# Two edits of a two-layer diffusion backbone: column-group sums of the modulation accumulators, and last down products with tokens on the partitions

## The chip, the cores and the metric

The kernel runs on one core of a Trainium2 chip. The metric is device time in microseconds (us) from launch to end. TensorE (PE) multiplies, VectorE (DVE) and ScalarE (ACT) work element by element, GpSimd (POOL) and SyncE (SP) mostly issue DMAs here. PE's weight loads have rows of their own (PEld). Every product of the bulk is done in three passes of a split float type, so that it has nearly float32 accuracy.

## The reference

Two layers over 256 latent tokens and 256 context tokens, 1024 channels each:

```python
# per layer; h = modulated RMSNorm; scale, shift and gate come from silu(c) @ w_mod + b_mod
x = x + 0.5 * gate1 * swiglu(h1, ffn1_w_gate, ffn1_w_up, ffn1_w_down)   # inner width 2816
x = x + gate_m * merge(token_mixers(h_m @ w_in), w_branch, w_out)
x = x + 0.5 * gate2 * swiglu(h2, ffn2_w_gate, ffn2_w_up, ffn2_w_down)
# after layer 1:
out = x * rsqrt(mean(x * x, axis=-1) + 1e-6) * final_norm               # latent tokens only
```

Context tokens go the same way with modulation vectors made from `c_ctx`. Behind the mixers of the last layer only latent tokens are left, so the last feed-forward block (ffn2 of layer 1) has 256 tokens.

## The kernel before

Activations lie with channels on partitions: `X` is 128 x 8 chunks x 512 tokens. Weights are handled in **units** of 128 x 1024 elements (512 KB). SP loads a unit into one of four `raw` slots. ACT copies it to `w_hi`, rounded to the split type (`split_hi`, L656), and DVE makes the rest `w_lo = raw - w_hi` (`split_lo`, L669). PE (`product`, L699) then does for each of its 8 rows of 128 channels two matmuls with `w_hi` as weights (L711 with the high part of the activations, L712 with their low part), and 8 more with `w_lo` (L717). `w_hi` and `w_lo` have two slots each: the unit after next can only be split when this one's matmuls have read them.

A feed-forward block has three **parts** of 8, 6 and 8 inner chunks (`PARTS`). A part is 16, 12 or 16 "up" units (gate and up products in turn, of h, with silu and product behind each pair) and then a "down" sweep of 8 units, one for each output chunk of 128 channels, with the part's inner chunks as rows. DVE adds each result times its gate to `X` (L1660). `inner_hi` comes from ACT (L1223) and `inner_lo` from DVE (L1622) behind each pair of up units. In the last sweep ACT also squares the new `X` chunk (L1173), POOL adds the squares up (L2112), and PE sums them over the partitions with a matrix of ones (L804, L806). Then follow the final norm (root, reciprocal, and the multiplication L1969), 16 transposes (L1161) that bring tokens to the partitions, four copies by ACT (L1545), and two DMAs out.

**Modulation.** silu(c) @ w_mod doesn't go over PE but for the first 16 chunks (`modulation`, L820, 32-column tiles on the four column groups of PE). The other 128 chunks, in 32 groups of 4, are loaded by POOL in the feed-forward blocks before they are needed. DVE multiplies and adds 8 rows of a group into `mac_acc` (`gstage` or `spread_odd`, L1645), for the context stream ACT scales (L1247) and POOL adds (L2019). What is left is to sum 128 partitions. `sum_macs` (L831) does it on PE behind fixed units (`sum_after`): for each chunk and stream one float32 matmul with 128 x 128 of the accumulator as weights and one column of ones as moving data (L847), which gives the 128 sums as a column of `bank[7]`. 24 groups have both streams (8 matmuls), 8 have one (4 matmuls). A float32 matmul is two records in the trace, one for each pass.

## Time and profile before

| | us |
|---|---|
| median of 3 runs (lowest to highest) | 2291.53 (2289.37 to 2294.31) |
| profiled execution, its own time | 2293.94 |
| its span in the trace | 2292.2 |
| PE busy, of the span | 2197.9 (96%) |
| DVE, ACT, POOL busy | 1473.0, 1006.3, 556.5 |
| DMA | 339.62 MB, mean 148 GB/s |

PE is busy nearly all the time, and its clock was granted at 0.986 of full speed on the mean. DVE is at 64% over the span. A row names the line of the kernel; for a matmul it reads out<-moving,weights. Start-to-start times of matmuls are the pace; a single matmul's own duration also has its latency and is longer than the pace.

### The profile page before, as it was taken

The numbers are of one execution on the slowest core, as the hardware profiler recorded it, in microseconds if no ns is written. First come the engines' busy times: TensorE is split into PE (matmuls) and PEld (weight loads), VectorE is DVE, ScalarE is ACT, GpSimd is POOL, SyncE is SP. The second block draws the span as 40 slices with busy tenths as digits, with TensorE's granted clock in tenths as the row PEclk, the third lists the DMA queues.
The fourth block names the chain that finished last, engine by engine and source line by source line (L and its number), as shares of the span: only waits on it lengthen the run. The fifth ranks groups of instructions, "written<-read, shape, count | busy, mean of one in ns | idle before, by whom it ended". The sixth has DMA issues, their size and how long they took to land. (4 is left out here: it accounts for less than half of the span.)

```text
span 2292.2 us, 32512 instructions
## 1 busy us (share of the span) xinstructions
PE 2197.9 (96%) x12273; PEld 1846.9 (81%) x12273; DVE 1473.0 (64%) x2102; ACT 1006.3 (44%) x1575; POOL 556.5 (24%) x566
## 2 busy tenths in 40 slices
PE   6999999999999988999999999999998999988998
PEld 3888888977666766988888898887888777888997
DVE  3877786783576457776666674445459558675554
ACT  3544444543455432553343453222245356634444
POOL 0556566420010011334443320000015001110000
PEclk8999999999999999999999999999999999999999
DMA  8566675633333335555445455545444445465663
GB/s 272 156 206 183 168 207 154 173 92 86 97 107 92 97 117 155 173 150 156 147 141 172 128 163 161 147 133 157 144 129 127 120 120 155 143 182 147 177 182 113
DMA packets 488576, 339.62 MB, mean 148 GB/s; under 512 B 13194, under 2 KB 460150, under 8 KB 488294
## 3 DMA queue, kind: packets, MB, share of 16 engines
q1 hardware_dynamic: 458240, 238.06, 36.3%
q0 software_dynamic: 28736, 95.30, 14.2%
q10 hardware_dynamic: 1446, 4.19, 0.5%
q8 instruction: 98, 1.61, 0.3%
q14 instruction: 56, 0.46, 0.1%
HBM read 325.92 MB, written 12.35 MB: 148 GB/s over the span
## 5 line engine op out<-in xcount | busy, mean ns | idle before, releaser
L677 DVE TENSOR_TENSOR w_lo<-raw,w_hi 128x1024 fp32r<-128x1024 f32 (+1 forms) x444 | 582.2, 1312 | 554.1 <-PE bank L717 363.1
L667 ACT ACTIVATE w_hi<-raw 128x1024 fp32r<-128x1024 f32 (+1 forms) x444 | 462.0, 1041 | 708.3 <-PE bank L712 372.3
L711 PE MATMUL bank<-h_hi,w_hi 128*128 128x512 f32 (+1 forms) x1856 | 647.3, 361 | 10.7 <-DVE h_lo L1559 10.6
L712 PE MATMUL bank<-h_lo,w_hi 128*128 128x512 f32 (+1 forms) x1856 | 639.0, 356 | 0.0
L711 PEld LDWEIGHTS bank<-h_hi,w_hi 128*128 128x128 f32 x1856 | 353.3, 190 | 63.4 <-issue 12.5
L717 PE MATMUL bank<-h_hi,w_lo 128*128 128x512 f32 (+1 forms) x1856 | 395.1, 355 | 3.7 <-DVE w_lo L677 3.7
L712 PEld LDWEIGHTS bank<-h_lo,w_hi 128*128 128x128 f32 x1856 | 353.7, 191 | 48.9 <-issue 0.5
L717 PEld LDWEIGHTS bank<-h_hi,w_lo 128*128 128x128 f32 x1856 | 313.8, 190 | 53.1 <-DVE w_lo L677 4.5
L711 PE MATMUL bank<-inner_hi,w_hi 128*128 128x256 f32 (+1 forms) x896 | 273.4, 327 | 11.9 <-DVE inner_lo L1622 11.6
L712 PE MATMUL bank<-inner_lo,w_hi 128*128 128x256 f32 (+1 forms) x896 | 270.4, 325 | 0.0
L711 PEld LDWEIGHTS bank<-inner_hi,w_hi 128*128 128x128 f32 x896 | 168.7, 188 | 31.1 <-DVE inner_lo L1622 15.8
L2000 POOL DMA_DIRECT2D wm<-in_w_mod_dram x128 | 92.8, 725 | 372.3 <-DVE gstage L1645 165.0
L726 PE MATMUL bank<-h_hi,w_hi 128*128 128x512 f32 (+1 forms) x512 | 169.7, 350 | 12.8 <-ACT wa L1418 7.7
L712 PEld LDWEIGHTS bank<-inner_lo,w_hi 128*128 128x128 f32 x896 | 168.4, 188 | 14.9
L727 PE MATMUL bank<-h_lo,w_hi 128*128 128x512 f32 (+1 forms) x512 | 165.1, 341 | 0.0
L717 PE MATMUL bank<-inner_hi,w_lo 128*128 128x256 f32 (+1 forms) x896 | 165.0, 324 | 0.0
L717 PEld LDWEIGHTS bank<-inner_hi,w_lo 128*128 128x128 f32 x896 | 135.2, 188 | 15.3
L1223 ACT ACTIVATE inner_hi<-wb 128x512 fp32r<-128x512 f32 (+1 forms) x88 | 50.9, 579 | 217.2 <-DVE wb L1618 217.2
L726 PEld LDWEIGHTS bank<-h_hi,w_hi 128*128 128x128 f32 x512 | 98.5, 192 | 47.2 <-ACT gstage L1418 19.1
L1645 DVE SCALAR_TENSOR_TENSOR gstage<-wm,cact,gstage 128x512 f32<-128x512 f32 x112 | 126.2, 1126 | 2.3
L1645 DVE SCALAR_TENSOR_TENSOR spread_odd<-wm,cact,spread_odd 128x512 f32<-128x512 f32 x112 | 123.3, 1101 | 2.3
L1660 DVE SCALAR_TENSOR_TENSOR X<-bank,gatev,X 128x256 f32<-128x256 f32 x192 | 87.9, 478 | 54.9 <-PE bank L717 54.9
(241 smaller groups left out, 2918.3 us busy)
## 6 DMA issues: line engine op xcount, KB each, us to landing
wm<-in_w_mod_dram POOLq DMA_DIRECT2D x128, 512.0 KB, 4.1
raw<-in_w_in_dram SPq DMA_DIRECT2D x108, 512.0 KB, 3.8
raw<-in_ffn_w_gate_dram SPq DMA_DIRECT2D x88, 512.0 KB, 4.3
raw<-in_ffn_w_up_dram SPq DMA_DIRECT2D x88, 512.0 KB, 3.9
raw<-in_ffn_w_down_dram SPq DMA_DIRECT2D x88, 512.0 KB, 4.0
raw<-in_ffn_w_down_dram SPq DMA_DIRECT2D x32, 384.0 KB, 3.4
raw<-in_w_out_dram SPq DMA_DIRECT2D x24, 512.0 KB, 4.0
raw<-in_w_mod_dram SPq DMA_DIRECT2D x16, 512.0 KB, 5.9
```

The lines of the kernel that those rows point to most:

```text
L667: act.activation(w_hi[n % 2][:, 0:unit.rows, :], raw[unit.slot][:, 0:unit.rows, :], ACT.Copy).then_inc(hi_made, 1)
L677: dve.tensor_tensor(w_lo[n % 2][:, 0:unit.rows, :], raw[unit.slot][:, 0:unit.rows, :], w_hi[n % 2][:, 0:unit.rows, :].bitcast(F32), ALU.su ...
L711: pe.matmul(psum, w_hi[s][:, row0 + k, :], hi, start=(k == 0), stop=False)
L712: mm = pe.matmul(psum, w_hi[s][:, row0 + k, :], lo, start=False, stop=False)
L717: mm = pe.matmul(psum, w_lo[s][:, row0 + k, :], rhs(k)[0], start=False, stop=(k == rows - 1))
L726: pe.matmul(psum, w_hi[s][:, k, :], h_hi[:, k, 0:n], start=(k == 0), stop=False)
L727: mm = pe.matmul(psum, w_hi[s][:, k, :], h_lo[:, k, 0:n], start=False, stop=False)
L1223: act.activation(inner_hi[:, bass.ds(i * 2 + j // 2, 1), 0:n], wb[:, (j // 2) % 2:(j // 2) % 2 + 1, 0:n], ACT.Copy).then_inc(inner_hi_made, 1)
L1645: ins = dve.scalar_tensor_tensor(out=acc, in0=row, scalar=cact[:, k, 0:1], in1=acc, op0=ALU.mult, op1=ALU.add)
L1660: ins = dve.scalar_tensor_tensor(out=X[:, d % DC, stream_cols(st)], in0=bank[4 + d % 2][:, stream_cols(st)], scalar=gatev[:, gate_i, d % D ...
L2000: wm_loaded[i % 3].done(pool.dma_start(wm[i % 3][:, :, :], w_mod[layer].rearrange("(k p) n -> p k n", p=P)[:, 2 * h:2 * h + 2, chunk * P:( ...
```

## The change

Two edits at once. **Sums.** `sum_macs` now issues four float32 matmuls per group, with 32 columns of ones as weights on the four column groups of PE and 256 columns (128 where there is one stream) of the accumulator as moving data; they fill `bank[6]` with rows of sums. One unit later ACT copies `bank[6]` to `mac_rows` (`copy_rows`), and one more unit later PE turns the rows to columns of `bank[7]` with two matmuls (one for one stream) of 128 x 128 as weights and 4 (8) columns of `pick8` (`turn_macs`).

**Last down products.** In ffn2 of layer 1 the down products have tokens on the partitions of the result. The activations (`inner_hi`, `inner_lo`, 128 tokens of one inner chunk) are the weights and 512 output channels of `w_hi` or `w_lo` the moving data. A unit is 2 inner chunks x 512 channels (half of the 1024), 8 + 6 + 8 = 22 units in place of 24. Four banks (two token halves by two channel halves) collect over all three parts, so that nothing is added to `X`. `X` itself is turned to tokens by 16 transposes before the block (`turn_residual`) and copied to `res` by ACT. At the end DVE multiplies by the gate row, adds `res` and multiplies by the final norm's row, ACT squares with a sum along the free axis, and both scale by the inverse root. The gate row and norm row are spread over the partitions by POOL's DMAs (`last_rows`), one through DRAM.

```diff
...
+def by_tokens(l, name):
+    return l == LAYERS - 1 and name in [(2, part) for part in range(len(PARTS))]
 def sweep_steps(l, name):
-    return DC * sweep_halves(l, name)
+    return PARTS[name[1]][1] if by_tokens(l, name) else DC * sweep_halves(l, name)
...
+            res = sb("res", [P, 2, D], F32, region)
+            gate_all = sb("gate_all", [P, D], F32, region)
+            fin_all = sb("fin_all", [P, D], F32, region)
...
+        RES_BANKS = [(1, 1, 3), (0, 0, 4), (0, 1, 5), (1, 0, 7)]
+        def token_units(l, part):
+            rows = PARTS[part][1]
+            return [(first["down", l, 2, part] + j, j // (rows // 2), j % (rows // 2)) for j in range(rows)]
+        scaled = (gstage, spread_odd)
...
+        mac_rows = (probs[:, 2, :], probs[:, 3, :])
-                sum_after.setdefault(u0 + int(pace * (i + 1)) + 2, []).append(g)
+                at_unit = u0 + int(pace * (i + 1)) + 2
+                sum_after.setdefault(at_unit, []).append(g)
+                copy_after.setdefault(at_unit + 1, []).append(g)
+                turn_after.setdefault(at_unit + 2, []).append(g)
...
+                        if by_tokens(l, (ffn, part)):
+                            for u, half, a in token_units(l, part):
+                                unit = units[u]
+                                sp.wait_ge(lo_made, units[u - SLOTS].product + 1)
+                                sp.dma_start(raw[unit.slot][:, :, :].rearrange("p r c -> p (r c)").rearrange("p (k n) -> p k n", k=2),
+                                             wd[l].rearrange("(c p) n -> p c n", p=P)[:, c0 + 2 * a:c0 + 2 * a + 2, half_cols(half)]
+                                             ).then_inc(loaded[unit.slot], 16)
+                            continue
...
             def sum_macs(u):
                 for g in sum_after.get(u, ()):
+                    n = GROUP * P // 2 if 1 in group_streams(g) else P
+                    mac_dve.wait(pe, (g, DC - 1))
+                    if 1 in group_streams(g):
+                        mac_pool.wait(pe, (g, DC - 1))
+                    if g > 0:
+                        pe.wait_ge(mac_rows_copied, g)
+                    for j in range(4):
+                        if 1 in group_streams(g):
+                            acc = mac_acc[g % 2][:, j % 2, :].rearrange("p (b h c) -> p b h c", b=2, h=2)[:, :, j // 2, :]
+                        else:
+                            acc = mac_acc[g % 2][:, 0, j * P:(j + 1) * P]
+                        mm = pe.matmul(bank[6][32 * j:32 * j + 32, 0:n], const("ones")[:, 0:32], acc, start=True, stop=True)
+                    mac_summed.done(mm, g)
+            def turn_macs(u):
+                for g in turn_after.get(u, ()):
                     l, chunk0 = MAC_GROUPS[g]
                     if g == 0:
                         vectors.wait(pe, (0, "in"))
...
                         vectors.wait(pe, (0, "gate"))
                     elif (l, chunk0) == (1, 5 * DC):
                         vectors.wait(pe, (1, "in"))
-                    mac_dve.wait(pe, (g, DC - 1))
+                    pe.wait_ge(mac_rows_copied, g + 1)
+                    c = mod_col(chunk0, 0)
                     if 1 in group_streams(g):
-                        mac_pool.wait(pe, (g, DC - 1))
-                    for s in group_streams(g):
-                        for q in range(GROUP):
-                            col = mod_col(chunk0 + q, s)
-                            mm = pe.matmul(bank[7][:, col:col + 1], mac_acc[g % 2][:, s, q * P:(q + 1) * P], const("ones")[:, 0:1],
+                        for b in range(2):
+                            mm = pe.matmul(bank[7][:, c + 4 * b:c + 4 * b + 4], mac_rows[g % 2][:, b * P:(b + 1) * P], const("pick8")[:, 0:8:2],
                                            start=True, stop=True)
-                    mac_summed.done(mm, g)
+                    else:
+                        mm = pe.matmul(bank[7][:, c:c + 8], mac_rows[g % 2][:, 0:P], const("pick8"), start=True, stop=True)
+                    mac_turned.done(mm, g)
...
+            def turn_residual(l):
+                pe.wait_ge(added, add_first[l, "out"] + sweep_steps(l, "out"))
+                vectors.wait(pe, (l, "rest"))
+                for t, half, b in RES_BANKS:
+                    for k in range(4):
+                        mm = pe.transpose(bank[b][:, k * P:(k + 1) * P], X[:, 4 * half + k, t * P:(t + 1) * P], const("ident"))
+                    res_turned.done(mm, b)
+            def down_by_tokens(l, part):
+                rows = PARTS[part][1]
+                last_part = part == len(PARTS) - 1
+                before = inner_first[l, 2, part]
+                if part == 0:
+                    pe.wait_ge(res_copied, len(RES_BANKS))
+                for u, half, a in token_units(l, part):
+                    s = units[u].product % 2
+                    wide_hi, wide_lo = (w[s][:, :, :].rearrange("p r c -> p (r c)").rearrange("p (k n) -> p k n", k=2) for w in (w_hi, w_lo))
+                    pe.wait_ge(hi_made, units[u].product + 1)
+                    last = last_part and a == rows // 2 - 1
+                    def hi_terms(t):
+                        for k in range(2):
+                            c = 2 * a + k
+                            if half == 0 and t == 0:
+                                pe.wait_ge(inner_lo_made, before + c + 1)
+                            begin = part == 0 and c == 0
+                            pe.matmul(bank[4 + 2 * t + half][:, :], inner_hi[:, c, t * P:(t + 1) * P], wide_hi[:, k, :], start=begin, stop=False)
+                            mm = pe.matmul(bank[4 + 2 * t + half][:, :], inner_lo[:, c, t * P:(t + 1) * P], wide_hi[:, k, :], start=False, stop=False)
+                        return mm
+                    def lo_terms(t):
+                        for k in range(2):
+                            c = 2 * a + k
+                            mm = pe.matmul(bank[4 + 2 * t + half][:, :], inner_hi[:, c, t * P:(t + 1) * P], wide_lo[:, k, :], start=False,
+                                           stop=last and k == 1)
+                        return mm
+                    if last:
+                        pe.wait_ge(lo_made, units[u].product + 1)
+                        hi_terms(0)
+                        tokens_done.done(lo_terms(0), (0, half))
+                        hi_terms(1).then_inc(hi_used, 1)
+                        mm = lo_terms(1)
+                    else:
+                        hi_terms(0)
+                        hi_terms(1).then_inc(hi_used, 1)
+                        pe.wait_ge(lo_made, units[u].product + 1)
+                        lo_terms(0)
+                        mm = lo_terms(1)
+                    mm.then_inc(unit_done, 1)
...
-            for t in range(2):
-                for half in range(2):
-                    for k in range(4 * half, 4 * half + 4):
-                        if t == 0:
-                            normed.wait(pe, ("final", k))
-                        mm = pe.transpose(bank[2 * t + half][:, (k % 4) * P:(k % 4 + 1) * P], X[:, k, t * P:(t + 1) * P], const("ident"))
-                    pe_start.done(mm, ("out", t, half))
...
+            def copy_rows(u):
+                for g in copy_after.get(u, ()):
+                    n = GROUP * P // 2 if 1 in group_streams(g) else P
+                    mac_summed.wait(act, g)
+                    if g >= 2:
+                        mac_turned.wait(act, g - 2)
+                    act.activation(mac_rows[g % 2][:, 0:n], bank[6][:, 0:n], ACT.Copy).then_inc(mac_rows_copied, 1)
+            def copy_residual(at_bank):
+                t, half, b = RES_BANKS[at_bank]
+                res_turned.wait(act, b)
+                act.activation(res[:, t, half_cols(half)], bank[b][:, :], ACT.Copy).then_inc(res_copied, 1)
+            def square_tokens(t, half):
+                res_added.wait(act, (t, half))
+                res_squared.done(act.activation(wa[:, t, :], res[:, t, half_cols(half)], ACT.Square, accum_out=ssq[:, t, half:half + 1]), (t, half))
+            def token_splits(l, part):
+                last_part = part == len(PARTS) - 1
+                for j, (u, half, a) in enumerate(token_units(l, part)):
+                    if last_part and j == 0:
+                        act.activation(early_root[:, 7:8], eps_col[:, 0:1], ACT.Sqrt)
+                    split_hi(act, units[u].product + 2)
+                    if last_part and j in (4, 5):
+                        square_tokens(j - 4, 0)
+                if last_part:
+                    for t in range(2):
+                        square_tokens(t, 1)
+                        res_summed.wait(act, t)
+                        res_root.done(act.activation(ssq[:, t, 2:3], ssq[:, t, 2:3], ACT.Sqrt, bias=eps_col[:, 0:1], scale=1.0 / D), t)
+                        res_inverse.wait(act, t)
+                        res_scaled.wait(act, (t, 0))
+                        act.activation(res[:, t, half_cols(0)], scaled[0][:, t, :], ACT.Identity, scale=ssq[:, t, 3:4]).then_inc(acts_finished, 1)
...
                 for i in range(PARTS[part][1] // 2):
+                    body(i)
                     if (l, ffn, part, i) == (0, 1, 0, 3):
                         modulation_vectors(0, "gate")
...
+            def add_tokens(t, half):
+                if (t, half) == (0, 0):
+                    row_loads.wait(dve, "all")
+                    dve.wait_ge(res_copied, len(RES_BANKS))
+                if t == 0:
+                    tokens_done.wait(dve, (t, half))
+                else:
+                    dve.wait_ge(unit_done, token_units(LAYERS - 1, 2)[4 * half + 3][0] + 1)
+                part = res[:, t, half_cols(half)]
+                gated.done(dve.tensor_tensor(wb[:, t, :], bank[4 + 2 * t + half][:, :], gate_all[:, half_cols(half)], ALU.mult), (t, half))
+                gated.wait(dve, (t, half))
+                res_added.done(dve.tensor_tensor(part, part, wb[:, t, :], ALU.add), (t, half))
+                res_added.wait(dve, (t, half))
+                res_scaled.done(dve.tensor_tensor(scaled[half][:, t, :], part, fin_all[:, half_cols(half)], ALU.mult), (t, half))
+            def finish_tokens(t):
+                res_squared.wait(dve, (t, 1))
+                res_summed.done(dve.tensor_tensor(ssq[:, t, 2:3], ssq[:, t, 0:1], ssq[:, t, 1:2], ALU.add), t)
+                res_root.wait(dve, t)
+                res_inverse.done(dve.reciprocal(ssq[:, t, 3:4], ssq[:, t, 2:3]), t)
+                res_inverse.wait(dve, t)
+                res_scaled.wait(dve, (t, 1))
+                dve.tensor_scalar(res[:, t, half_cols(1)], scaled[1][:, t, :], ssq[:, t, 3:4], None, ALU.mult).then_inc(dves_finished, 1)
+            def token_block(l, part):
+                last_part = part == len(PARTS) - 1
+                for j, (u, half, a) in enumerate(token_units(l, part)):
+                    if last_part and j in (4, 5):
+                        add_tokens(j - 4, 0)
+                    split_lo(dve, units[u].product + 2)
+                if last_part:
+                    for t in range(2):
+                        add_tokens(t, 1)
+                        if t == 1:
+                            finish_tokens(0)
+                    finish_tokens(1)
...
-            norm_invert(("final", 0), 0)
-            for k in range(DC):
-                normed.done(dve.scalar_tensor_tensor(out=X[:, k, 0:LAT], in0=X[:, k, 0:LAT], scalar=vec2[:, 0, V_FIN + k:V_FIN + k + 1],
-                                                     in1=rstd[:, 0:LAT], op0=ALU.mult, op1=ALU.mult), ("final", k))
...
+            def last_rows():
+                gate_row_stored.done(pool.dma_start(last_gates.rearrange("(c p) -> p c", p=P), gatev[:, 2, :, 0], allow_slow_non_contiguous=True), 0)
+                row_loads.done(pool.dma_start(fin_all[:, :], final_norm.rearrange("(a d) -> a d", a=1).to_broadcast([P, D])), 0)
+                gate_row_stored.wait(pool, 0)
+                row_loads.done(pool.dma_start(gate_all[:, :], last_gates.rearrange("(a d) -> a d", a=1).to_broadcast([P, D])), "all")
```

Below, what stands on PE and DVE at the places that matter. PE behind up unit 6 of the first part of ffn1, layer 0, before:

```order
L712 MATMUL bank<-h_lo,w_hi 128x512
L717 MATMUL bank<-h_hi,w_lo 128x512 x8
L847 MATMUL bank<-cst,gstage 128x1 x8
L711 MATMUL bank<-h_hi,w_hi 128x512
L712 MATMUL bank<-h_lo,w_hi 128x512
```

and in the change (line numbers are the new ones; `cst` holds the ones and `pick8`, `probs` holds `mac_rows`), first behind the same unit, then two units later:

```order
L766 MATMUL bank<-h_lo,w_hi 128x512
L771 MATMUL bank<-h_hi,w_lo 128x512 x8
L899 MATMUL bank<-gstage,cst 32x256 x4
L765 MATMUL bank<-h_hi,w_hi 128x512
L766 MATMUL bank<-h_lo,w_hi 128x512
```

```order
L766 MATMUL bank<-h_lo,w_hi 128x512
L771 MATMUL bank<-h_hi,w_lo 128x512 x8
L916 MATMUL bank<-cst,probs 128x4 x2
L765 MATMUL bank<-h_hi,w_hi 128x512
L766 MATMUL bank<-h_lo,w_hi 128x512
```

Eight matmuls of one moving column have become four of 256 columns on 32-column tiles, and two of four columns two units later.

The end of DVE's program, before (the last down sweep's end, then the final norm):

```order
L677 TENSOR_TENSOR w_lo<-raw,w_hi 128x1024
L1660 SCALAR_TENSOR_TENSOR X<-bank,gatev,X 128x256
L677 TENSOR_TENSOR w_lo<-raw,w_hi 128x1024
L1660 SCALAR_TENSOR_TENSOR X<-bank,gatev,X 128x256 x3
L1573 RECIPROCAL rstd<-rstd 128x256
L1969 SCALAR_TENSOR_TENSOR X<-X,vec,rstd 128x256 x8
```

and in the change, from the split of unit 6 of the last sweep's units 0 to 7:

```order
L731 TENSOR_TENSOR w_lo<-raw,w_hi 128x1024
L1845 TENSOR_TENSOR wb<-bank,gate_all 128x512
L1847 TENSOR_TENSOR res<-res,wb 128x512
L1849 TENSOR_TENSOR gstage<-res,fin_all 128x512
L731 TENSOR_TENSOR w_lo<-raw,w_hi 128x1024
L1845 TENSOR_TENSOR wb<-bank,gate_all 128x512
L1847 TENSOR_TENSOR res<-res,wb 128x512
L1849 TENSOR_TENSOR spread_odd<-res,fin_all 128x512
L1845 TENSOR_TENSOR wb<-bank,gate_all 128x512
L1847 TENSOR_TENSOR res<-res,wb 128x512
```

The additions of three whole 128 x 512 operations each now stand between the last splits and behind the last products; a reciprocal of 128 x 256 and eight multiplications are gone from the end.

## Rows read from the trace of the kernel before

**Rows 1.** The page: busy time and share of PE, and its granted clock in tenths.
```profile
PE 2197.9 (96%) x12273; PEld 1846.9 (81%) x12273; DVE 1473.0 (64%) x2102; ACT 1006.3 (44%) x1575; POOL 556.5 (24%) x566
...
PEclk8999999999999999999999999999999999999999
```
**Rows 2.** Stretch of ffn1, layer 0: busy PE, PEld, DVE, ACT, POOL, clock, DMA share, GB/s.
```profile
60.00:130.00 70.00, 69.98 (x347) 59.17 (x346) 60.63 (x57) 37.81 (x55) 40.24 (x32) 1.00 0.59 173
```
**Rows 3.** Timeline of PE at a group with two streams: start, us, engine, line, what.
```profile
93.46 1.84 PE L847 MATMUL bank<-cst,gstage 128*128 128x1 f32 x16
95.16 0.49 PE L711 MATMUL bank<-h_hi,w_hi 128*128 128x512 f32 x1
95.48 0.40 PE L712 MATMUL bank<-h_lo,w_hi 128*128 128x512 f32 x1
```
**Rows 4.** Timeline of PE, L717 of two units in turn, then a one-stream group.
```profile
1651.38 1.98 PE L717 MATMUL bank<-h_hi,w_lo 128*128 128x512 f32 x8
...
1656.82 1.98 PE L717 MATMUL bank<-h_hi,w_lo 128*128 128x512 f32 x8
1658.64 0.95 PE L847 MATMUL bank<-cst,gstage 128*128 128x1 f32 x8
```
**Rows 5.** Timeline of PE at the start: float32 passes, then four tiled matmuls.
```profile
40.97 0.38 PE L804 MATMUL bank<-wb,cst 128*128 128x256 f32 x1
41.19 0.59 PE L806 MATMUL bank<-wa,cst 128*128 128x256 f32 x2
41.71 1.07 PE L820 MATMUL bank<-raw,cact 128*32 128x512 f32 x8
```
**Rows 6.** Timeline of PE into and out of 64-column tiles; out of 64-row tiles.
```profile
680.52 0.39 PE L727 MATMUL bank<-h_lo,w_hi 128*128 128x512 f32 x1
680.83 0.64 PE L1088 MATMUL bank<-mod_row,x_tok 128*64 128x512 f32 x1
...
681.84 2.12 PE L736 MATMUL bank<-h_hi,w_lo 128*128 128x512 f32 x8
...
623.90 0.50 PE L726 MATMUL bank<-h_hi,w_hi 128*128 128x512 f32 x1
624.24 0.39 PE L727 MATMUL bank<-h_lo,w_hi 128*128 128x512 f32 x1
```
**Rows 7.** Timeline of PE in ffn2, layer 1: last L717 before each down sweep and in it.
```profile
2128.97 1.12 PE L717 MATMUL bank<-h_hi,w_lo 128*128 128x256 f32 x8
...
2153.33 1.12 PE L717 MATMUL bank<-inner_hi,w_lo 128*128 128x256 f32 x8
...
2187.88 1.12 PE L717 MATMUL bank<-h_hi,w_lo 128*128 128x256 f32 x8
...
2206.83 0.88 PE L717 MATMUL bank<-inner_hi,w_lo 128*128 128x256 f32 x6
...
2252.66 1.12 PE L717 MATMUL bank<-h_hi,w_lo 128*128 128x256 f32 x8
2256.80 0.39 PE L711 MATMUL bank<-inner_hi,w_hi 128*128 128x256 f32 x1 [1.35 <-DVE inner_lo L1622]
...
2277.75 1.12 PE L717 MATMUL bank<-inner_hi,w_lo 128*128 128x256 f32 x8
```
**Rows 8.** Groups by form on DVE and ACT: busy us, mean ns, idle before.
```profile
L1618 DVE TENSOR_TENSOR wb<-bank,wa 128x512 f32<-128x512 f32 x66 | 45.1, 683 | 0.0
...
L1852 DVE RECIPROCAL smax<-smax 128x1 f32<-128x1 f32 x72 | 11.7, 162 | 3.9 <-ACT probs L1444 1.3
...
L1446 ACT ACTIVATE smax<-sink,smax 128x1 f32<-128x1 f32 x24 | 6.8, 283 | 0.0
```
**Rows 9.** Timeline of DVE at the start of the last down sweep.
```profile
2254.28 1.23 DVE L677 TENSOR_TENSOR w_lo<-raw,w_hi 128x1024 fp32r<-128x1024 f32 x1 [1.82 <-ACT w_hi L667]
```
**Rows 10.** Chain of waits, its last piece: start, us, what.
```profile
2288.46 0.60 ACT out_rows L1545
```
**Rows 11.** Timeline of PE behind the output projection of layer 1.
```profile
2081.17 0.55 PE L784 MATMUL bank<-h_hi,w_hi 128*128 128x256 f32 x1 [4.15 <-DVE h_lo L1588]
```

73 lines of the change are left out of this document (54 added, 19 removed).

## The prediction

> **What bounds the kernel now.** I read the page first: PE is busy 96% of the span at a clock granted near full speed all along [rows 1]. So whatever shortens PE's own program is worth nearly all of itself, and an edit on another engine is worth nothing unless PE waits for it. Next the stretches: in ffn1 of layer 0, where the modulation groups lie thickest, PE is busy 69.98 of 70.00 us, DVE 60.63 (87%), ACT 37.81 (54%), the DMA engines 0.59 [rows 2]. PE sets the time there, but DVE isn't far. Then PE's timeline at the sums, at other changes of tile shape, and in ffn2 of layer 1, and last the end of the program, where PE has stopped and a chain of DVE, ACT and DMA is left.
>
> **Sums, removed.** At a two-stream group PE starts the first L847 at 93.46 and the next product at 95.16: 1.70 us for 16 records. The product's second matmul then comes 0.32 later [rows 3], where the pace is 5.44 / 24 = 0.227 (two L717 rows one unit apart, 1651.38 and 1656.82) [rows 4]: 0.10 more. That is 1.80 for a group. The busy time of those 16 records, 1.84, is 0.14 longer than the 1.70. At a one-stream group 8 records have 0.95 [rows 4], less 0.14 that is 0.81, with the 0.10 it is 0.91. All: 24 x 1.80 + 8 x 0.91 = 50.5 us. A record more costs (1.70 - 0.81) / 8 = 0.111.
>
> **Sums, added.** Do float32 matmuls on four column groups run beside each other? L820 does just this at the start: four matmuls of 512 columns with 32 columns of weights, 8 records, in 1.07 us, the last one's latency included [rows 5]. A pass of 256 columns on the whole array takes 41.19 - 40.97 = 0.22, so one of 512 takes 0.43, and 8 in turn would be 3.4 us. So they do. The price of the change of shape comes from the 64-column products: the last 128-column matmul starts at 680.52 and the first tiled one at 680.83, 0.31 and not 0.227, so 0.08 for going in; two passes of 512 columns then take 681.84 - 680.83 = 1.01 [rows 6], of which 0.15 is more than 2 x 0.43 and goes to the turnovers, the way out among them. After a way out, the next matmul but one is late as well, 624.24 - 623.90 = 0.34 for 0.227, 0.11 more [rows 6]. A group with two streams thus costs 0.08 + (2 x 0.22 + 0.15) + 0.11 = 0.78, and I add 0.02 for four tiles that can't start in the same instant: 0.80. The turn two units later is 4 records of the old kind: 1.70 - 12 x 0.111 = 0.37, and 0.10 behind it, 0.47. Sum 1.27 for 1.80, a gain of 0.53. With one stream: 0.08 + (2 x 0.11 + 0.15) + 0.11 + 0.02 = 0.58, and a turn of 2 records, 0.14 + 0.10: 0.82 for 0.91, a gain of 0.09. Together 24 x 0.53 + 8 x 0.09 = **13.4 us**. The bounds: if ways in and out cost nothing, a group is 0.34 cheaper still (11 us in all); if the four tiles run one after the other, the first rival below.
>
> The Trainium skill has a rule against this edit (TensorEngine Tiling (Array Packing), Tiling Modes): changing the tiling mode drains the engine. It gives no time for it. The trace agrees that there is a price, 0.08 in and some 0.2 out [rows 6], which the sum holds already. The same page's table (Overview) promises up to 4x for a dimension of 32 or less, and rows 5 show it.
>
> What else the edit adds: ACT copies 128 x 256 or x 128 per group, at most the 0.60 of a whole 512 [rows 10], 32 times in stretches where ACT is 46% idle [rows 2]; PE asks for the copy two units, 10.9 us, after the sums, so I cost it at nothing. If ACT were a unit late, each group would lose what it is late, which is the price if that cover is gone. DVE waits for the turn, not the sum, before it makes the vectors, but does so four units after the last turn it needs. The "gate" vectors move behind an up pair on DVE; the same work, before the sweep that uses them. Behind them DVE still has a whole unit (5.44) before the split is due. Queues of SP and POOL aren't moved past anything here.
>
> **Last down products, sweeps.** Three sweeps [rows 7]. Part 0: L717 of the last up unit starts at 2128.97, that of the last down unit at 2153.33, 24.36. Part 1: (2206.83 + 6 x 0.12) - (2187.88 + 8 x 0.12) = 18.71. In the change a unit is 12 matmuls of 512 columns, 12 x 0.227 = 2.72 us: 8 units 21.8, 6 units 16.3. Gain 2.6 + 2.4. It has two sources. 512 columns take 0.227, twice 256 take 0.24. And the old sweep's first unit needs all inner chunks at once, so it waits for the last `inner_lo`: 1.35 us of it in the last part [rows 7], somewhat over 1 in the others. The new first units need chunks 0 and 1 only; the last pair is asked for at the fourth (third) unit, 5 us or more later. Nothing takes that place. Of a unit's 2.72 DVE needs 1.23 for its split [rows 9], and it no longer adds to `X`.
>
> **The last sweep and the end.** Now from the end of up, 2252.66 + 8 x 0.12 = 2253.62, to 2292.2: 38.6 us. In the change, from that zero: unit 7 could start at 7 x 2.72 = 19.0. But unit 7 waits for its whole split before it starts, and DVE now has two additions of three operations of 0.68 [rows 8] between its last splits: it splits for unit 5 once unit 3 (done at 10.9) has gone and ACT has made the high part (11.8 to 13.0, by [rows 9]), adds to 15.1, splits for unit 6 to 16.3, adds to 18.3, splits for unit 7 to 19.5. So unit 7 starts at **19.5**, half a us late. Its first token half is done at 19.5 + 6 x 0.227 + 0.2 = 21.1, and DVE's three operations for it end at 23.2; the second half waits for them, to 25.2. Then the sum of squares (0.16), ACT's root (0.28), the inverse (0.16) [rows 8] with four handovers, 25.9; ACT scales in 0.60 [rows 10], 26.5. ACT's order puts the last square behind that: 27.1, sum, root and inverse again 27.8, scaled 28.4. From the last ACT operation to the span's end it was 2292.2 - (2288.46 + 0.60) = 3.1 [rows 10], with the same size of DMA: 31.5. Gain 38.6 - 31.5 = **7.1**. DVE's and ACT's tail is what is late next.
>
> **The turn of the residual.** 16 transposes are put where PE waits 4.15 us for the first `h_lo` (until 2081.17) [rows 11]. At the higher clock 128 float32 columns take 0.11 (half of 256 in [rows 5]), at the lower one 0.22, so they need 1.8 to 3.5 us. They fit. If they don't, it costs up to 1 us; if they keep the clock up, it gives a few tenths back. ACT copies them beside the first up units, 4 x 0.60 in 11 us. POOL's three DMAs have 170 us until they are needed.
>
> **Sum.** 13.4 + 2.6 + 2.4 + 7.1 = 25.5. From the profiled execution, 2293.94 - 25.5 = 2268.4. That execution was 2.4 above the median of the runs, so the median to expect is 2291.53 - 25.5 = **2266.0**.
>
> **Rivals.**
> - *The column groups don't overlap in this form.* Then a two-stream group has 8 passes of 0.22 in turn, 1.76 + 0.34 for the shapes + 0.47 = 2.57, and loses 0.77; a one-stream group has 0.88 + 0.34 + 0.24 = 1.46 and loses 0.55. 24 x 0.77 + 8 x 0.55 = 22.9 lost, 12.1 gained elsewhere: 2291.5 + 10.8 = 2302, slower. It decides once the four tiled matmuls of a two-stream group take over some 1.8 us and not 0.8. Rows 5 speak against it: same type, same weights' width, one bank. Chance 0.04.
> - *The sums' gain is hidden*, since DVE's multiply-and-adds set the pace once PE is quicker. For it: 87% in rows 2. Against: PE waited 0.02 of 70 us there, and DVE's share only rises to 89%. Then only 12.1 is left: 2279. Chance 0.07.
> - *The token sweeps don't gain*: splits come late, or the end's chain is as long as the old one. Then 13.4 and some: 2277. Chance 0.07. Against it: DVE is at less than half a unit in the sweeps.
> - *Neither does what it says* and the time stays within 0.2% (about what a measurement of this kernel can tell from no change): 0.02.
> - My forecast, both terms within a third of their size: 0.80.
>
> Faster by over 0.2% holds all but the first rival and the fourth, 0.94; slower 0.04. The range: 2260, where ways in and out cost half of what I take and the end is 1 us shorter, to 2276, where one of the two middle rivals is half true.
>
> **What would show it.** In the profile after: four tiled matmuls (8 records) in about 0.6 us and no L847; no wait of PE for `mac_rows` copies; down units of layer 1's ffn2 2.72 apart, with no gap at the first; PE idle under 1 us before the last unit; the last PE matmul of the last product some 9 us before the end, where it was 13.3. Wrong would be: tiled records one behind another, waits <-ACT `probs` on PE, or a clock below full in the last sweep.

## The result, and the profile after

| | before | after |
|---|---|---|
| median (lowest to highest), us | 2291.36 (2289.37 to 2294.31) | 2270.66 (2267.81 to 2273.47) |
| profiled execution, span | 2292.2 | 2266.0 |
| PE busy | 2197.9 | 2174.7 |

The ratio is 0.9909, with an interval of 0.9896 to 0.9922: 20.7 us faster, where I forecast 25.5. The spans differ by 26.2, but 5.1 of that lie before the first product (it starts at 48.69 before and 43.57 after), where the first loads come in; in the eleven kernels of the experiments it starts at 42.84 to 45.69. So I compare stretches from the first product on. Their bounds are the starts of the first matmuls of `first_pair` and `score`. So the first two columns hold the input products of a layer's mixers too, and "mixers" is what lies from a layer's first scores to its next feed-forward block. There neither edit touches anything but for the 16 transposes, which fill a wait. One execution each, us (differences in the text are of unrounded times):

| kernel | ffn1, layer 0 | ffn2 L0 and ffn1 L1 | mixers | last block to the end | sum |
|---|---|---|---|---|---|
| before | 546.7 | 898.2 | 587.6 | 211.0 | 2243.5 |
| after | 540.3 | 891.4 | 586.4 | 204.3 | 2222.4 |
| e1, sums alone | 541.0 | 890.9 | 584.8 | 210.6 | 2227.3 |
| e2, tokens alone | 545.8 | 898.3 | 585.4 | 204.2 | 2233.7 |
| e3, three more | 556.3 | 908.8 | 585.4 | 204.2 | 2254.7 |
| e4, banks | 540.3 | 889.7 | 585.8 | 204.2 | 2219.9 |
| e5, residual early | 540.5 | 891.4 | 586.1 | 200.7 | 2218.6 |
| e6, copy and vectors early | 537.4 | 891.3 | 585.3 | 203.1 | 2217.1 |
| e7, end order | 542.0 | 889.7 | 586.5 | 203.4 | 2221.6 |
| e8, 128 bytes on | 541.3 | 887.2 | 586.1 | 203.1 | 2217.6 |
| e9, all together | 536.4 | 888.6 | 584.4 | 199.0 | 2208.3 |
| e10, 256 bytes on | 540.3 | 891.4 | 586.0 | 203.0 | 2220.7 |
| e11, 64 bytes on | 540.9 | 888.1 | 585.4 | 203.5 | 2217.9 |

The 21.0 us between the first two rows are 6.4 + 6.8 in the stretches with the sums, 6.6 in the last block, and 1.2 that belongs to neither edit. The first two sections of the page after, beside [rows 1]:

```profile
PE 2174.7 (96%) x11925; PEld 1796.8 (79%) x11925; DVE 1474.5 (65%) x2085; ACT 1015.7 (45%) x1608; POOL 553.7 (24%) x563
...
PEclk9999999999999999999999999999999999999999
```

PE, at 96%, still bounds the kernel. Next the timeline of PE at the sums of one group and at the turn of another, which answers to [rows 3], and at the sums of a one-stream group:

```profile
88.40 0.64 PE L899 MATMUL bank<-gstage,cst 128*32 128x256 f32 x8
88.97 0.50 PE L765 MATMUL bank<-h_hi,w_hi 128*128 128x512 f32 x1
89.31 0.39 PE L766 MATMUL bank<-h_lo,w_hi 128*128 128x512 f32 x1
...
124.80 0.51 PE L916 MATMUL bank<-cst,probs 128*128 128x4 f32 x4
125.16 0.48 PE L765 MATMUL bank<-h_hi,w_hi 128*128 128x512 f32 x1
...
1638.80 0.42 PE L899 MATMUL bank<-gstage,cst 128*32 128x128 f32 x8
1639.16 0.50 PE L765 MATMUL bank<-h_hi,w_hi 128*128 128x512 f32 x1
```

Eight records of 256 columns are over in 0.57 us and the next matmul but one is 0.11 late (89.31 - 88.97 = 0.34). The turn has 0.36. That is the mechanism that I forecast, to 0.04 us. But at two groups of the first block PE waits for something. These are rows of DVE, ACT and PE around the first of them, and PE's row at the second:

```profile
98.67 0.68 DVE L1775 TENSOR_TENSOR wb<-bank,wa 128x512 f32<-128x512 f32 x1
...
99.38 0.63 ACT L1344 ACTIVATE inner_hi<-wb 128x512 fp32r<-128x512 f32 x1 [5.33 <-DVE wb L1775]
99.92 1.32 ACT L1409 ACTIVATE probs<-wm,cact 128x512 f32<-128x512 f32 x2
...
101.14 0.36 ACT L1360 ACTIVATE probs<-bank 128x256 f32<-128x256 f32 x1
...
101.65 0.58 PE L916 MATMUL bank<-cst,probs 128*128 128x4 f32 x4 [1.50 <-ACT probs L1360]
...
149.45 0.61 PE L916 MATMUL bank<-cst,probs 128*128 128x4 f32 x4 [0.94 <-DVE gatev L1895]
```

Read it from the bottom up. PE waits for ACT's copy L1360. ACT had been idle for 5.33 us, but the copy stands in its order behind `inner_hi`, which needs DVE's `wb`, and behind two scalings. This is one of the signs that the prediction had named for being wrong ("waits <-ACT `probs` on PE"), at one of 32 turns. The second wait, at 149.45, is for the "gate" vectors, which the change moved behind DVE's last multiply-and-adds of the part. In the last block the timeline of PE shows the largest wait:

```profile
2057.30 3.01 PE L958 MATMUL bank<-cst,X 128*128 128x128 f32 x16
2061.66 0.36 PE L838 MATMUL bank<-h_hi,w_hi 128*128 128x256 f32 x1 [1.35 <-DVE h_lo L1745]
...
2072.10 1.12 PE L771 MATMUL bank<-h_hi,w_lo 128*128 128x256 f32 x8
2075.25 0.38 PE L765 MATMUL bank<-h_hi,w_hi 128*128 128x256 f32 x1 [2.03 <-ACT res L1366]
...
2077.78 1.91 PE L771 MATMUL bank<-h_hi,w_lo 128*128 128x256 f32 x8
```

The 16 transposes fit in the gap, as forecast. But the fourth up unit needs bank 3, out of which ACT has not yet copied the residual. ACT's timeline shows what stands ahead of that copy (L1366):

```profile
2070.05 1.28 ACT L1341 ACT_TABLE_LOAD   x1
...
2074.30 0.42 ACT L1344 ACTIVATE inner_hi<-wb 128x256 fp32r<-128x256 f32 x1 [1.63 <-DVE wb L1775]
2074.62 0.58 ACT L1366 ACTIVATE res<-bank 128x512 f32<-128x512 f32 x1
```

It stands behind `inner_hi`, which waits for DVE's `wb`, and ahead of both ACT loads a table for silu. And behind the wait the same eight matmuls take 1.91 us and not 1.12. The windows of that stretch (columns as in [rows 2]) show why: behind the wait the clock was granted at 0.50, which is 1.2 GHz.

```profile
2073.40:2075.20 1.80, 0.00 (x0) 0.00 (x0) 1.29 (x3) 0.90 (x3) 0.00 (x0) 1.00 0.66 197
2076.70:2079.90 3.20, 3.20 (x17) 3.20 (x16) 0.81 (x2) 1.26 (x2) 0.00 (x0) 0.50 0.42 116
```

Now two token units in turn on PE, beside the sweeps in [rows 7]:

```profile
2118.92 1.08 PE L986 MATMUL bank<-w_lo,inner_hi 128*128 128x512 f32 x4
...
2121.70 1.10 PE L986 MATMUL bank<-w_lo,inner_hi 128*128 128x512 f32 x4
```

A unit takes 2.79 us on the mean, not 2.72. Last the chain of waits at the end, which answers to [rows 10]:

```profile
2258.86 0.69 DVE spread_odd L1849
...
2259.65 0.30 ACT ssq L1386
...
2260.18 0.72 ACT res L1389
2260.90 0.62 ACT wa L1371 x2
...
2262.26 0.72 ACT res L1389
```

ACT's second square (L1371) stands behind its first scaling (L1389), as forecast, but has an instruction more behind it that reads the sum out (x2), and a scaling takes 0.72, not 0.60.

### The profile page after: what moved, and what is told of

Same layout as the page of the kernel before. It is cut to its first block and busy times, and to the rows that moved or that the text cites. A ratio compares the mean times of both kernels' runs of the same rounds, so it can differ in the third digit from the quotient of the medians.

```text
span 2266.0 us, 31839 instructions
## 1 busy us (share of the span) xinstructions
PE 2174.7 (96%) x11925; PEld 1796.8 (79%) x11925; DVE 1474.5 (65%) x2085; ACT 1015.7 (45%) x1608; POOL 553.7 (24%) x563
## 3 DMA queue, kind: packets, MB, share of 16 engines
q0 software_dynamic: 29056, 96.35, 14.5%
## 5 line engine op out<-in xcount | busy, mean ns | idle before, releaser
L765 PE MATMUL bank<-h_hi,w_hi 128*128 128x512 f32 (+1 forms) x1856 | 650.5, 362 | 13.1 <-DVE h_lo L1716 11.0
L765 PE MATMUL bank<-inner_hi,w_hi 128*128 128x512 f32 (+1 forms) x720 | 229.9, 340 | 7.7 <-DVE inner_lo L1779 7.4
L766 PE MATMUL bank<-inner_lo,w_hi 128*128 128x512 f32 (+1 forms) x720 | 225.7, 334 | 0.0
L765 PEld LDWEIGHTS bank<-inner_hi,w_hi 128*128 128x128 f32 x720 | 135.5, 188 | 28.8 <-DVE inner_lo L1779 11.0
L766 PEld LDWEIGHTS bank<-inner_lo,w_hi 128*128 128x128 f32 x720 | 135.6, 188 | 13.8
L771 PE MATMUL bank<-inner_hi,w_lo 128*128 128x512 f32 (+1 forms) x720 | 139.3, 334 | 0.0
L771 PEld LDWEIGHTS bank<-inner_hi,w_lo 128*128 128x128 f32 x720 | 112.1, 188 | 14.9
L1817 DVE SCALAR_TENSOR_TENSOR X<-bank,gatev,X 128x256 f32<-128x256 f32 x168 | 76.2, 477 | 49.5 <-PE bank L771 49.5
```

Source lines behind the costliest of these rows:

```text
L765: pe.matmul(psum, w_hi[s][:, row0 + k, :], hi, start=(k == 0), stop=False)
L766: mm = pe.matmul(psum, w_hi[s][:, row0 + k, :], lo, start=False, stop=False)
L771: mm = pe.matmul(psum, w_lo[s][:, row0 + k, :], rhs(k)[0], start=False, stop=(k == rows - 1))
L1817: ins = dve.scalar_tensor_tensor(out=X[:, d % DC, stream_cols(st)], in0=bank[4 + d % 2][:, stream_cols(st)], scalar=gatev[:, gate_i, d % D ...
```

## The experiments

**Each edit alone (e1, e2).** e1 is the kernel before with the diff's `sum_macs`, `turn_macs` and `copy_rows`, and its place for the "gate" vectors; e2 is the changed kernel with the old sums:

```diff
-                        turn_macs(u0 + 4 * i + j)
                         sum_macs(u0 + 4 * i + j)
...
-                        copy_rows(u0 + 4 * i + j)
```

> The kernel before with the sums edit alone. Theory A (the edit gives 0.57 us for each of 24 two-stream groups and 0.09 to 0.14 for 8 one-stream groups, 14.5 in all, and two waits of PE at turns in ffn1 of layer 0 take 2.75 back): 11.7 us faster than before, with both waits there. Rival B (the groups' gain is real, but DVE falls behind and gives some of it back elsewhere, so the shortfall of the whole change sits here): 8 to 9 us faster, with waits on DVE that the changed kernel shows in other places than these two.

> The changed kernel with the old modulation sums. Theory A (sweeps give 2.2 and 2.0, the last sweep with the end 6.5, and the late copy of the residual costs 3.8): 6.9 to 7.5 us faster than before, with PE waiting 2 us before the fourth up unit of the last block and its clock at half speed behind it. Rival B (the wait comes from the sums edit's shift of DVE's or ACT's work): no such wait, and 10 to 11 us faster.

Measured: e1 2274.42, ratio 0.9928 (0.9915 to 0.9942), 16.8 faster; e2 2282.12, 0.9965 (0.9951 to 0.9979), 9.1 faster. PE's timeline of e1 at the first turn of the sums that waits:

```profile
102.82 0.58 PE L868 MATMUL bank<-cst,probs 128*128 128x4 f32 x4 [1.50 <-ACT probs L1262]
```

And PE's timeline of e2 at the fourth up unit of the last block:

```profile
2087.37 0.38 PE L759 MATMUL bank<-h_hi,w_hi 128*128 128x256 f32 x1 [2.03 <-ACT res L1331]
```

Both kernels have the waits of the changed kernel, to a hundredth of a us (e1 has the second one too, at 150.62). So theory A is right on the places, and each wait belongs to its own edit. Its sizes are too small by the medians. By the table e1 gains 5.7 + 7.3 in the stretches that its edit touches and e2 6.7 in the last block. The rest (2.7 and 2.2 us) lies in the mixers, and 0.8 of e2's in its other stretches, where the sums are the old ones; the last part says where that comes from. The mixers take from 584.4 to 587.6 in these thirteen executions. PE often waits there, and the places where its clock is granted at half differ from run to run. That the two medians add up to 25.9 and the whole change has 20.7 is in part this; e7 below shows another part.

**What the column groups are worth (e3).**

```diff
-                    for j in range(4):
+                    for j, at_group in [(1, 0), (2, 0), (3, 0), (0, 0), (1, 1), (2, 2), (3, 3)]:
...
-                        mm = pe.matmul(bank[6][32 * j:32 * j + 32, 0:n], ...
+                        mm = pe.matmul(bank[6][32 * at_group:32 * at_group + 32, 0:n], ...
```

> The changed kernel, and ahead of each group's four tiled matmuls three more of the same shape, all on the first column group; the four behind them write over what they leave. Theory A (tiles on one group follow each other, tiles on four groups run side by side): 6 passes of 0.22 more for a two-stream group and 6 of 0.11 for a one-stream one, 24 x 1.32 + 8 x 0.66 = 37 us slower than the changed kernel. Rival B (a tiled matmul is cheap because of its 32 columns of weights, and not for running beside others): 6 records at 0.57 / 8 = 0.07 each, 0.43 a group, 10 to 13 us slower.

Measured: 2301.03, 30.4 slower than the changed kernel by the medians; by the table 16.0 in the first stretch and 17.4 in the second. Its timeline of PE at a group:

```profile
87.72 1.91 PE L899 MATMUL bank<-gstage,cst 128*32 128x256 f32 x14
89.56 0.50 PE L765 MATMUL bank<-h_hi,w_hi 128*128 128x512 f32 x1
```

1.84 us for 14 records where 8 had 0.57: the six on one group cost 0.21 each, and the eight on four groups 0.07 each. Rival B falls. 24 x 1.27 and 8 x 0.6 would be 35. Ten two-stream and the eight one-stream groups lie in the second stretch: 17.5 by these prices, 17.4 measured. The first stretch, with 14 two-stream groups, has 16.0 for 17.8. In part that is the wait at 101, 0.22 and not 1.50, because PE comes later to that turn and finds the copy nearly made. The other 0.5 I can't place.

**The banks (e4).**

```diff
+        bank = bank[4:] + bank[:4]
```

> The changed kernel with the eight PSUM banks numbered from the fifth on (banks 0 to 3 and 4 to 7 trade places), nothing else. Down products take 0.232 to 0.234 us for a matmul of 512 columns in both kernels, up products 0.227. Theory A (the pace goes with what is multiplied, inner_hi and inner_lo, or with their place in the memory): down products stay at 0.232 to 0.234, up products at 0.227, and the time stays within 3 us. Rival B (banks 4 to 7 are the slower ones): down products fall to 0.227 and up products rise to 0.233; with more 512-column up matmuls than down ones the kernel gets some 8 us slower.

Measured: 2267.05, ratio 0.9897 (0.9882 to 0.9912); down products still 0.232 on the mean, up products 0.227, token units 2.79 apart. The banks aren't it. The median is 3.6 under the changed kernel's, a little more than theory A allowed; the profiled executions differ by 2.5, and e7 shows where 1.7 of that come from.

**The residual's copy (e5).**

```diff
+                if by_tokens(l, (ffn, part)) and part == 0:
+                    copy_residual(0)
+                    copy_residual(1)
...
-                        if by_tokens(l, (ffn, part)) and part == 0 and 1 <= 4 * i + j <= 4:
-                            copy_residual(4 * i + j - 1)
+                        if by_tokens(l, (ffn, part)) and part == 0 and 2 <= 4 * i + j <= 3:
+                            copy_residual(4 * i + j)
```

> The changed kernel with ACT's first two copies of the residual at the head of its part of the last block (ahead of the split for the third unit), where ACT waits 1.39 us for PE; the other two stay behind units 2 and 3. Theory A (PE's 2.03 us before the fourth up unit come from the place of the first copy in ACT's order, and the half clock behind it from that wait): no wait there, the clock stays at full speed through units 3 and 4, and from the first product of the last block to the end of the program it takes 200.5 us, where the changed kernel takes 204.3; 3.8 us faster. Rival B (the clock falls there anyway): 2.3 us gained and the unit behind still takes over 4 us, 202.0.

Measured: 2265.37, ratio 0.9885 (0.9868 to 0.9901), and 200.7 us for the last block to the end, where theory A said 200.5. ACT's timeline ahead of the first up units:

```profile
2068.30 1.06 ACT L1369 ACTIVATE res<-bank 128x512 f32<-128x512 f32 x2
2069.91 1.06 ACT L721 ACTIVATE w_hi<-raw 128x1024 fp32r<-128x1024 f32 x1 [0.55 <-issue]
```

And PE's at the third and fourth:

```profile
2073.03 1.12 PE L771 MATMUL bank<-h_hi,w_lo 128*128 128x256 f32 x8
2073.99 0.28 PE L765 MATMUL bank<-h_hi,w_hi 128*128 128x256 f32 x1
...
2075.91 1.12 PE L771 MATMUL bank<-h_hi,w_lo 128*128 128x256 f32 x8
```

The two copies fill ACT's idle time, PE goes on at once, and a unit is 2.88 us (2075.91 - 2073.03) at the full clock. So the half clock came from the wait: PE was 2.3 us late, and it cost 3.7. The wait doesn't always have that price. Nine of the profiled kernels have it at this place, 2.03 or 2.04 us long. In seven the clock is at 0.50 behind it; in e6 and e10 it is not, and their last block takes 203.1 and 203.0 us, not 204.3. The stretch behind the wait in e6:

```profile
2074.10:2077.30 3.20, 3.20 (x29) 3.20 (x29) 1.99 (x3) 1.24 (x2) 0.00 (x0) 1.00 0.43 125
```

**The copy of the sums and the "gate" vectors (e6).**

```diff
                         split_hi(act, ...)
+                        copy_rows(u0 + 4 * i + j)
...
-                        copy_rows(u0 + 4 * i + j)
...
+                        if (l, ffn, part, i, j) == (0, 1, 0, 3, 1):
+                            modulation_vectors(0, "gate")
                         multiply_add(u0 + 4 * i + j)
...
-                    if (l, ffn, part, i) == (0, 1, 0, 3):
-                        modulation_vectors(0, "gate")
```

> The changed kernel with ACT's copy of the sums ahead of its wait for the pair's product and ahead of the scaling of rows, and the 'gate' vectors of layer 0 on DVE behind unit 13 of the first part, not behind its last multiply-and-adds. Theory A (each of PE's two waits comes from what stands ahead of that one step on ACT and on DVE): both waits go, and from the first product to the scores of layer 0 it takes 540.3 - 2.7 = 537.6 us. Rival B (DVE is late there as a whole and makes PE wait for a split or a multiply-and-add in its stead, as the kernel with three matmuls more, where the first wait is gone, may be read): 539 or more, with new waits of PE on DVE between 95 and 150 us.

Measured: 2264.96, ratio 0.9883 (0.9867 to 0.9900), and 537.4 us from the first product to the scores, where theory A said 537.6. PE's timeline at the turn that waited:

```profile
99.39 1.98 PE L771 MATMUL bank<-h_hi,w_lo 128*128 128x512 f32 x8
...
101.20 0.51 PE L916 MATMUL bank<-cst,probs 128*128 128x4 f32 x4
```

DVE and ACT are as late as before (`wb` at 99.88, `inner_hi` at 100.59), and PE no longer asks.

**The order of the end (e7).**

```diff
                     for t in range(2):
                         square_tokens(t, 1)
+                    for t in range(2):
                         res_summed.wait(act, t)
                         res_root.done(...)
+                    for t in range(2):
                         res_inverse.wait(act, t)
...
-                        if t == 1:
-                            finish_tokens(0)
-                    finish_tokens(1)
+                    for t in range(2):
+                        sum_tokens(t)
+                    for t in range(2):
+                        invert_tokens(t)
+                    for t in range(2):
+                        finish_tokens(t)
```

> The changed kernel with both sums of squares ahead of both roots at the end: ACT squares, squares, root, root, scales, scales; DVE sums, sums, inverts, inverts, scales, scales. Theory A (ACT's second square behind its first scaling is what sets the end): the last scaling starts at some 60.9 us on the clock on which it started at 62.26, and the last matmul is 8.3 us before the end and not 9.64. Rival B (the output DMAs on SP's queue, one behind the other, set it): the last scaling is early and the end within 0.4 us of where it was.

Measured: 2268.54, ratio 0.9896 (0.9879 to 0.9912). In its timeline the scalings and the DMAs' issues are

```profile
2262.25 1.33 ACT L1392 ACTIVATE res<-gstage,ssq 128x512 f32<-128x512 f32 x2
...
2263.00 0.97 SPq L704 DMA_DIRECT2D out_dram<-res  x2
```

The last matmul starts 8.86 us before the end, where it was 9.69 (the expectation counts from 0.05 later). The last scaling starts 1.45 us earlier behind that matmul, somewhat more than theory A said, but only 0.83 of them are left at the end. The DMA view says where they went. In the changed kernel the two transfers of 512 KB stood apart, each 2.61 us from issue to landing. Now they are issued 0.61 us apart and run behind one another without a gap at 403 to 429 GB/s, and the second takes 3.25. Rival B has that part.

The run shows a second thing. It, too, waits 1.49 us at the turn, and its windows behind the wait read

```profile
98.00:105.50 7.50, 6.01 (x29) 4.74 (x29) 6.73 (x8) 4.00 (x7) 4.43 (x4) 1.00 0.81 246
105.70:109.00 3.30, 3.30 (x9) 2.61 (x8) 3.27 (x3) 0.72 (x1) 2.68 (x3) 0.50 0.33 61
```

where the changed kernel's profiled run keeps 1.00. Hence the 1.7 us more of its first stretch. e8 and e11 have the same fall, e1, e4, e5 and e10 have not, with the same wait. So a wait of 1.5 us costs the clock in some executions and not in others. The profiled run of the changed kernel was spared there, but hit at another place. At the input products of layer 1's mixers PE waits 1.98 us in all thirteen profiled kernels. In six, the changed one, e3, e5, e6, e9 and e10, the clock is at 0.50 from about that wait's end:

```profile
1762.70:1765.90 3.20, 3.20 (x9) 2.46 (x8) 1.48 (x2) 2.85 (x5) 0.00 (x0) 0.50 0.70 184
```

e4 and e7 have the same program there and keep 1.00, and their second stretch takes 889.7 and not 891.4. So the same 1.7 us are lost at one place or the other, or, as in e4, at neither. The profiled run, 2267.81, is the fastest of its four all the same, and their median is 2.9 above it. Its mean granted clock is 0.987, that of the other three 0.986, 0.985 and 0.985. More such falls are the likely cause, but those three executions have no trace, so it isn't shown. e4 and e10, which change only places in memory, have 2267.05 and, from a single run, 2267.34. So some 3 us of the distance between 25.5 and 20.7 may be the changed kernel's four executions and not its program.

**The place of `inner_hi` and `inner_lo` (e8, e10, e11).** One row of padding ahead of them, 32, 64 or 16 floats:

```diff
+            pad = sb("pad", [P, 32], F32, region)
             inner_hi = sb("inner_hi", [P, 8, TOK], F32R, region)
```

> The changed kernel with inner_hi and inner_lo (and what follows them) 128 bytes further on in each partition, nothing else. Theory A (the place of these tensors against that of the weights is what makes their matmuls take 0.232 us and not 0.227): token units 2.72 us apart and not 2.79, and 512-column down products of the other blocks at 0.227. Rival B (it goes with something else, such as the loads of the down weights that run beside them): 0.232 as before, and the same time.

> The changed kernel with inner_hi and inner_lo 256 bytes further on. They then start at a multiple of 256 bytes again, as in the changed kernel, where the weights and h start at 128 over a multiple of 256. Theory A (what counts is the place modulo 256 bytes): 0.232 us for their matmuls, as in the changed kernel. Rival B (any move off the old place does it, by what neighbours it or by what is shared with it): 0.227.

> The changed kernel with inner_hi and inner_lo 64 bytes further on, so they start at 64 over a multiple of 256 bytes and the weights at 128. Theory A (the operands of a matmul have to start at the same place modulo 256, or at any rate 128 over it): 0.231 to 0.234 us. Rival B (only a start at a multiple of 256 is slow; the kernel before, which starts at 224 over one and is slow, speaks against it): 0.227.

Measured: e8 2261.01 (two runs; ratio 0.9863, 0.9844 to 0.9883), e10 2267.34 and e11 2265.01 (a single run each). Two token units on PE, first of e8:

```profile
2118.59 1.07 PE L987 MATMUL bank<-w_lo,inner_hi 128*128 128x512 f32 x4
2121.31 1.07 PE L987 MATMUL bank<-w_lo,inner_hi 128*128 128x512 f32 x4
```

Of e10:

```profile
2118.48 1.08 PE L987 MATMUL bank<-w_lo,inner_hi 128*128 128x512 f32 x4
2121.26 1.10 PE L987 MATMUL bank<-w_lo,inner_hi 128*128 128x512 f32 x4
```

Of e11:

```profile
2116.77 1.07 PE L987 MATMUL bank<-w_lo,inner_hi 128*128 128x512 f32 x4
2119.52 1.07 PE L987 MATMUL bank<-w_lo,inner_hi 128*128 128x512 f32 x4
```

They are 2.72, 2.78 and 2.75 apart. The means of one matmul, start to start, in token units and in the down products of the first two stretches, which have 512 or 256 columns:

| start of `inner_hi` over a multiple of 256 bytes | token, 512 | down, 512 | down, 256 |
|---|---|---|---|
| 224 (before) | | 0.2334 | 0.1200 |
| 0 (after, e10) | 0.2323 | 0.2326 | 0.1187 |
| 64 (e11) | 0.2289 | 0.2333 | 0.1146 |
| 128 (e8) | 0.2271 | 0.2273 | 0.1199 |

The last column goes another way. Two down units of 256 columns in e11, 2.73 us apart where the 24 matmuls of such a unit take 2.88 in e8:

```profile
395.80 1.08 PE L772 MATMUL bank<-inner_hi,w_lo 128*128 128x256 f32 x8
398.53 1.07 PE L772 MATMUL bank<-inner_hi,w_lo 128*128 128x256 f32 x8
```

Weights and `h` start at 128. Theory A holds in e8 and e10; in e11 the token units are better than it said, the 512-column down products as it said. No expectation asked about 256 columns: there 64 is the best of the four, 4% under 128, and by the table e11 as a whole takes no longer than e8 (2217.9 and 2217.6). A move by itself does nothing (e10). Whether the operands have to match, or a start is good by itself, and why the two widths differ, stays open. The Trainium skill (SBUF — State Buffer, Operand start alignment) asks only for a start at a multiple of the element's size and calls that legality, not speed. All these starts keep that rule, and here the start does have a price, up to 3% at 512 columns and 5% at 256.

**All together (e9).** The edits of e5, e6, e7 and e8.

> The changed kernel with the four edits that moved something by themselves: residual copies early, copies of the sums and 'gate' vectors early, the order of the end, and inner_hi and inner_lo 128 bytes on. Theory A (they lie in different places and add up): from the first product to the end 2222.4 us less 2.9, 3.7, 0.8 and 6.1, 2208.9 us, and some 2254 to 2257 us as a median. Rival B (with the waits gone DVE sets the time in ffn1 of layer 0, and the faster down products there are waited away): 2211 to 2213 us from the first product, with new waits on DVE in that block.

Measured: 2254.36 (2252.55 to 2257.89), ratio 0.9832 (0.9819 to 0.9846), and 2208.3 from the first product, where theory A said 2208.9. That it came within 0.6 is in part luck. The 6.1 for the padding held the 1.7 us of half clock in the changed kernel's second stretch, which e8 doesn't have and e9 has again; without them the sum is 2210.6. The mixers, which no edit touches, took 2.0 less than in the changed kernel. Its window over ffn1 of layer 0, beside [rows 2]:

```profile
60.00:130.00 70.00, 69.99 (x328) 56.97 (x327) 61.41 (x52) 39.26 (x56) 43.74 (x35) 1.00 0.66 182
```

PE waits 0.01 of 70 us there. DVE, at 88%, does not set the time. This version beats both kernels, by 38.6 and 16.3 us.

## Why the prediction was right, and where it was off

The direction, the size within the range and the main mechanisms were right. Term by term, in us:

| term | forecast | measured | from |
|---|---|---|---|
| sums | 13.4 | 13.2 (e1: 13.0) | first two stretches |
| sweeps of parts 0 and 1 | 5.0 | 4.0 | end of up to end of down, 24.36 to 22.30 and 18.71 to 16.73 |
| last sweep and end | 7.1 | 6.5 | 38.6 to 32.1 |
| turn of the residual | 0 | -3.7 | e5 |
| sum | 25.5 | 20.0 | |

1.2 us of the mixers makes it 21.2; 0.2 is rounding and the bounds of the stretches.

*The turn of the residual* is the step that failed: "ACT copies them beside the first up units, 4 x 0.60 in 11 us". I counted ACT's time and not its order. The copies fit; the first came too late because it stood behind `inner_hi`, and that behind DVE's `wb` and, ahead of that, ACT's load of a table for silu. I had also asked nothing about who needs bank 3, though PE's wait for the copy stands in the diff. The prediction priced only transposes that don't fit, at up to 1 us. And in the profiled run the price was 1.4 us more than PE's delay, through the clock; in e6 and e10 it was not.

*The sums.* Every piece came out within 0.04: 0.09 for the way in (forecast 0.08), 0.57 + 0.11 (0.61 + 0.11), the turn 0.36 + 0.09 (0.47). A two-stream group gains 0.57, not 0.53. Two steps failed, each at one of 32 turns. "PE asks for the copy two units, 10.9 us, after the sums, so I cost it at nothing" is the same mistake as above: I had named the price, not the case. And for the "gate" vectors I had asked only when DVE's next split is due, not that a turn of PE waits for them. They cost 1.7 + 1.1, and e6 gives it back (2.9).

That the term still came out at 13.2 for 13.4 is luck. By its pieces the edit is worth 24 x 0.57 + 8 x 0.1 = 14.5, less 2.8, and 0.7 of shorter waits at the first down products of layer 0's ffn1 (a gap of 1.97 became 1.53) and of its ffn2 (2.23 to 1.99): 12.4. e1, with this edit alone, has 13.0; 0.6 stay open. In the changed kernel two things come on top that aren't the sums'. The token edit's new tensor `ssq` takes 32 bytes and so moves `inner_hi` from 224 to 0 over a multiple of 256. By the table of places that is 0.0013 us for each of 1152 down matmuls of 256 columns and 0.0008 to 0.0010 for each of 1008 of 512, some 2.4 us; e2, which has the token edit alone, shows 0.9 of it in its first stretch; its second has a stretch of half clock of its own, at 1303.5. Against it stand the 1.7 us of half clock at the input products of layer 1. 12.4 + 2.4 - 1.7 = 13.1.

*The sweeps.* The count of matmuls, and that no first unit waits, were right. The duration was taken from the wrong row: [rows 4] are up products at 0.227, and 0.233 is what 512-column matmuls with `inner` had, in the kernel before too. With e8's padding the unit is the forecast 2.72.

*The last sweep and the end.* The stall before the last unit (0.5 forecast) is a gap of 0.48, some 0.25 over the pace; with units 2.79 apart the last unit starts 19.8 us after the up products, where I had 19.5. From there the chain went as forecast but for ACT's two prices: 0.72 for the scaling, where I took 0.60, and 0.19 for reading the accumulator, which I had left out.

*The rivals.* Column groups that don't overlap: e3 shows the overlap and its price. DVE as the bound: e9 speaks against it. Token sweeps without gain: no, at 4.0 of 5.0.

## What to carry to other kernels

When a step is put on an engine that has time, write down what stands ahead of it in that engine's own order and what that waits for. Here ACT was idle 55% of the time and made PE wait twice, and DVE, at 65%, a third time. Put such a step ahead of the engine's next wait; e5 and e6 needed nothing else. Take a matmul's duration from a row with the same operands, not only the same shape. And before you read a difference of 1 or 2 us between two profiles, compare the stretches in which each had the clock at half: here one such stretch was worth 1.7 us, in some executions of the same code and not in others.

## What the runs showed of the hardware

- Four float32 matmuls on four column groups, 256 columns each: 0.57 us for 8 records; on one group each further record costs 0.21. The change of tile shape costs PE 0.09 on the way in and 0.11 at the second matmul after.
- A wait of PE of 2.03 us between full-speed work was followed by a granted clock of 0.50 for over 3 us in seven of nine profiled executions, though PE was busy again by then, and that cost 1.2 to 1.4 us of 256-column matmuls. A wait of 1.98 us, with two of 1.54 ahead of it, was followed by the same in six of thirteen, and a wait of 1.5 us in three of eight; each cost 1.7 us of 512-column ones.
- The start of an operand in its partition sets the pace of a matmul: 0.227 to 0.233 us at 512 columns and 0.1146 to 0.1200 at 256, and the best start isn't the same for both.
- ACT's square with a sum along the row is followed by a read of the accumulator of 0.19 us (0.63 + 0.19 for 512 elements).
- Two output transfers of 512 KB issued 0.61 us apart ran one behind the other at 403 to 429 GB/s; the second took 3.25 us to land and not 2.61, so 0.6 us of an earlier start were lost.
